# Low parts of the first block's weights on GpSimd instead of VectorE, in a two-block float32 network

## The chip, the cores and the metric

The kernel runs on one core of a Trainium2 chip. The metric is the time on the device in microseconds (us), from the start to the end of one execution. The core has TensorE (matrix products), VectorE (DVE), ScalarE (ACT), GpSimd (POOL) and SyncE (SP). Each works through its own queue in order; they wait for one another by semaphores. SBUF is the memory on chip, PSUM holds the results of TensorE.

## The reference

Two blocks of two layers each, on 512 tokens of width 1024, in float32. The change touches the first block alone. A layer of it is:

```python
h = rms_norm(x, norm_g)
z = h @ w_in
(fq, fk, fv, ff, f_gate, glu_in, c_gate,
 nq, nkc, nvc, nks, nvs, nkw, nvw, n_gl, n_gate) = jnp.split(z, split_points, axis=-1)
o_a = fox_attention(...) * jax.nn.silu(f_gate)
o_b = conformer_conv(...) * jax.nn.silu(c_gate)
o_c = nsa_attention(...) * jax.nn.silu(n_gate)
mixed = jnp.concatenate([o_a, o_b, o_c], axis=-1)
return x + mixed @ w_out
```

`fox_attention` is causal softmax attention with a decay; `conformer_conv` has 31 taps on each of 256 channels; `nsa_attention` has three branches, one over compressed keys and two of plain softmax. The second block (four mixers, gates and an MLP) is only of interest for what its trace shows.

## The kernel before

**Products in three passes.** TensorE multiplies in a one-pass float32 format with fewer bits. Each operand is split into a high part (rounded by a copy on ScalarE) and a low part (the difference), and a product is the sum of high x high, high x low and low x high (`three_passes`, L790: lines L794 to L796). The weights come from DRAM, so each tile of weights needs this at run time: `split_high` (L771, the copy at L775) on ScalarE and `split_low` (L777, the subtraction at L781, written to `w_low`) on VectorE, after a wait for the high part.

**The stream.** The large products of a layer, `h @ w_in` and `mixed @ w_out`, form a stream of 45 units (class `Inward`, L804): 29 of kind "z" for `w_in`, each one tile of up to 128 output rows and 1024 deep (24 matmuls), and 16 of kind "out" for `w_out`, each 512 deep (12 matmuls; s is the half of the depth, e the tile of the output). Weights have three slots. `fetch` (L761) on ScalarE's queue waits until the unit that used the slot is multiplied, then loads; `split_high(i + 1)` comes right behind the fetch of unit i + 2. TensorE waits for `w_low(i)` and for its PSUM bank, which VectorE's `drain` (L930; L942 for "z", L938 for "out") or, for rows with rotary embedding, the first step of `rotate_dve` (L725) frees.

**Woven with the mixers.** A unit is cut into pieces of two steps of depth. Each engine's program of the stream is a Python generator that is advanced one piece at a time (`go_on`, L637). `Stage.beside` (L324) writes a mixer's instructions into the same five queues, and after each step of the mixer's TensorE program, by a share that the mixer names, a piece of the stream. So VectorE's queue holds mixers' instructions and the stream's in the order in which they were written, and one that waits holds up all behind it. The mixers are Fox (with `Taps`: the convolution's taps on VectorE, L1614, four instructions at a step), then `ConvAndCompress`, then `Nsa`. After Nsa the rest of the stream (the second half of "out") runs by `finish` (L651), which writes each engine's remaining program to its end.

**GpSimd.** In the first block the mixers give it only two small products a layer (L1998, after waits for TensorE at L1958). The stream's `pool` (L798) yields once for each piece and then writes `total_pool` (L382): six adds at L389 that sum the squares of x (made by ScalarE at L380 as the last units are drained). TensorE sums the total over partitions (L393, L395), ScalarE makes the root (L407, L409), and a barrier ends the layer.

**Lines used below.** L562/L565 `gained_dve`: low parts of h. L744 `row_lo`. L1492: masking and maximum of Fox's scores, from PSUM. L1508: copy of transposed probabilities from PSUM. L1658: Fox's output of a tile. L1716: Fox's last transposes. L2033: GELU's scaling in the compression. L1350: low parts of the MLP's hidden values in the second block, on GpSimd. L3186, L3192, L3795: GpSimd's products in the second block's mixers. L2880: taps of the second block, on VectorE.

Of the kernel before, what the change touches and what calls it, by code (L numbers as in the profile page):

```python
# [8 lines left out]
F32 = mybir.dt.float32  # L9
F32R = mybir.dt.float32r  # L10
ACT = mybir.ActivationFunctionType
ALU = mybir.AluOpType
# [245 lines left out]
class Stage:  # L258
# [43 lines left out]
    def act(self):  # L302
        yield

    def dve(self):
        yield

    def pool(self):
        yield
# [296 lines left out]
class Woven(Stage, Gained):  # L606
# [170 lines left out]
    def split_low(self, i):  # L777
        if i < len(self.units):
            s, n, d = i % self.SLOTS, self.width(i), self.depth(i)
            self.v.wait_ge(*self.w_high(i))  # L780
            self.v.tensor_tensor(self.wl[s][:, 0:d, 0:n], self.w[s][:, 0:d, 0:n], self.wh[s][:, 0:d, 0:n].bitcast(F32),  # L781
                                 ALU.subtract).then_inc(self.w_low.sem, 1)
# [21 lines left out]
class Inward(Woven):  # L804
# [60 lines left out]
    def pe(self):  # L865
# [25 lines left out]
                yield  # L891
        self.root.sum_total_pe()

    def act(self):
        self.gained_act(range(2))
        self.split_high(0)
        self.gained_act(range(2, KD))
        for i, (kind, s, e) in enumerate(self.units):
            if kind == "z":
                yield  # L900
                self.fetch(self.a, i + 2)
                self.split_high(i + 1)
                if self.is_form(i - 2, "rope"):
                    self.row_high(i - 2)
                if self.is_form(i - 1, "split"):
                    self.row_high(i - 1)
                yield
                yield
                yield
                if i == self.kept - 1:  # L910
                    yield
            else:
                if e == 0:
                    for j in range(4):
                        self.a.copy(self.k.yT_low[:, 8 + 4 * s + j, :], self.k.yT[:, 4 * s + j, :]).then_inc(self.y_high.sem, 1)
                self.fetch(self.a, i + 2)
                self.split_high(i + 1)
                if s == 1 and e >= 2:
                    self.x_square(i - 2)
                yield  # L920
                yield
        for i in (-2, -1):
            self.x_square(len(self.units) + i)
        self.root.root_act()
# [19 lines left out]
    def dve(self):  # L944
        self.gain_dve(self.l)
        self.root.eps_dve()
        self.gained_dve(range(2))
        self.split_low(0)
        self.gained_dve(range(2, KD))
        for i, (kind, s, e) in enumerate(self.units):  # L950
            if i != 0 and i != self.kept:
                self.drain(i - 1)
            if kind == "z":
                yield
                yield
                self.split_low(i + 1)
                if self.is_form(i - 2, "rope"):
                    self.row_lo(i - 2)
                if self.is_form(i - 1, "split"):
                    self.row_lo(i - 1)  # L960
                yield
                self.rotate_dve(i - 1)
                yield
                if i == self.kept - 1:
                    self.drain(i)
                    yield
            else:
                if e == 0:
                    for j in range(4):
                        self.v.wait_ge(*self.y_high(s, j))  # L970
                        self.v.tensor_tensor(self.k.yT_low[:, 4 * s + j, :], self.k.yT[:, 4 * s + j, :],
                                             self.k.yT_low[:, 8 + 4 * s + j, :].bitcast(F32), ALU.subtract).then_inc(self.y_low.sem, 1)
                yield
                self.split_low(i + 1)
                yield
        self.drain(len(self.units) - 1)
        yield
# [2877 lines left out]
```

## Time and profile before

| | |
|---|---|
| Median of 3 runs | 3767.71 us (3763.28 to 3783.55) |
| The profiled execution | 3757.45 us, of which the span is 3755.6 us |
| Busy, share of the span | PE 92%, PEld 75%, DVE 56%, ACT 39%, POOL 11% |
| First block | 27 to 943 us, two passes (487 us is the border) |
| Mean of a 512-column matmul (L795) | 403 ns, overlapping the next |
| Units in the plain stream | 5.60 us apart ("z"), 2.80 us ("out"), by the starts of L942 and L938 |
| L1614, 128x512, first block | 120 recorded, mean 742 ns |

Times in the profile are us from the span's start. A row in order of time gives the start, the duration, the engine and line, out<-in, and in brackets how long the engine stood still before it and what ended that. A group gives busy time and the mean of one, then the engine's idle time before such instructions. Shares are means over stages with different limits.

### The profile page before, as it was taken

The numbers are of one execution on the slowest core, as the hardware profiler recorded it, in microseconds if no ns is written. First come the engines' busy times: TensorE is split into PE (matmuls) and PEld (weight loads), VectorE is DVE, ScalarE is ACT, GpSimd is POOL, SyncE is SP. The second block draws the span as 40 slices with busy tenths as digits, with TensorE's granted clock in tenths as the row PEclk, the third lists the DMA queues.
The fourth block names the chain that finished last, engine by engine and source line by source line (L and its number), as shares of the span: only waits on it lengthen the run. The fifth ranks groups of instructions, "written<-read, shape, count | busy, mean of one in ns | idle before, by whom it ended". The sixth has DMA issues, their size and how long they took to land. (4 is left out here: it accounts for less than half of the span.)

```text
span 3755.6 us, 48507 instructions
## 1 busy us (share of the span) xinstructions
PE 3441.2 (92%) x17756; PEld 2834.1 (75%) x17756; DVE 2089.3 (56%) x4082; ACT 1448.7 (39%) x2809; POOL 407.1 (11%) x322
## 2 busy tenths in 40 slices
PE   8889888898898998899999999899998999999998
PEld 6777767787587887677777887687887777777886
DVE  3756638466368883555763333478873656653333
ACT  3224332143444453444434232344453444433222
POOL 0000000000022221000202111032220000212111
PEclk9989999899899999999999999999999999999999
DMA  5633056330333323432433332433225242433332
GB/s 145 182 96 97 26 143 177 95 80 26 105 113 96 90 87 84 107 100 77 127 104 86 94 96 79 126 104 102 85 79 123 71 104 88 114 110 86 96 96 84
DMA packets 570478, 373.52 MB, mean 99 GB/s; under 512 B 77020, under 2 KB 500956, under 8 KB 569980
## 3 DMA queue, kind: packets, MB, share of 16 engines
q10 hardware_dynamic: 416768, 209.74, 20.4%
q1 hardware_dynamic: 153468, 160.59, 15.3%
q8 instruction: 148, 2.42, 0.3%
q14 instruction: 94, 0.77, 0.1%
HBM read 310.69 MB, written 59.57 MB: 99 GB/s over the span
## 5 line engine op out<-in xcount | busy, mean ns | idle before, releaser
L794 PE MATMUL bank<-h,w_hi 128*128 128x512 f32 (+2 forms) x2240 | 961.7, 429 | 124.9 <-DVE w_low L781 62.8
L796 PE MATMUL bank<-h,w_low 128*128 128x512 f32 (+2 forms) x2240 | 903.1, 403 | 0.0
L795 PE MATMUL bank<-h,w_hi 128*128 128x512 f32 (+2 forms) x2240 | 902.8, 403 | 0.0
L775 ACT CAST w_hi<-w 128x1024 fp32r<-128x1024 f32 (+2 forms) x456 | 434.4, 953 | 825.5 <-PE bank L796 661.2
L781 DVE TENSOR_TENSOR w_low<-w,w_hi 128x1024 fp32r<-128x1024 f32 (+2 forms) x456 | 507.9, 1114 | 395.2 <-ACT w_hi L775 395.0
L794 PEld LDWEIGHTS bank<-h,w_hi 128*128 128x128 f32 (+2 forms) x2240 | 430.9, 192 | 254.2 <-issue 87.6
L796 PEld LDWEIGHTS bank<-h,w_low 128*128 128x128 f32 (+2 forms) x2240 | 429.1, 192 | 107.7
L795 PEld LDWEIGHTS bank<-h,w_hi 128*128 128x128 f32 (+2 forms) x2240 | 431.7, 193 | 100.0 <-issue 13.0
L795 PE MATMUL bank<-yT_low,w_hi 128*128 128x512 f32 x768 | 305.4, 398 | 0.0
L1465 ACT ACTIVATE prob<-bank,softmax_stat 128x512 f32<-128x512 f32 (+3 forms) x256 | 144.9, 567 | 281.3 <-DVE softmax_stat L1499 204.4
L362 PE MATMUL bank<-v_tok,prob_T 128*128 128x64 f32 (+1 forms) x1376 | 188.3, 270 | 4.8 <-DVE y_tok L2154 2.1
L362 PEld LDWEIGHTS bank<-v_tok,prob_T 128*128 128x128 f32 x1376 | 176.3, 192 | 14.6 <-issue 10.7
L794 PE MATMUL bank<-yT_low,w_hi 128*128 128x512 f32 x384 | 157.6, 410 | 22.4 <-DVE xT L938 12.0
L1266 DVE TENSOR_TENSOR xT<-xT,bank 128x512 f32<-128x512 f32 x80 | 55.1, 688 | 216.9 <-PE bank L796 216.9
L795 PEld LDWEIGHTS bank<-yT_low,w_hi 128*128 128x128 f32 x768 | 146.2, 190 | 30.4
L1499 DVE TENSOR_REDUCE softmax_stat<-bank 128x1 f32<-128x128 f32 (+1 forms) x192 | 103.3, 552 | 104.3 <-PE bank L1425 103.9
L796 PE MATMUL bank<-yT_low,w_low 128*128 128x512 f32 x384 | 154.3, 402 | 0.0
L1273 DVE SCALAR_TENSOR_TENSOR relu<-bank,rstd 128x512 f32<-128x512 f32 x64 | 44.1, 692 | 185.4 <-PE bank L796 172.4
L3037 ACT COPY yT<-bank 128x512 f32<-128x512 f32 x96 | 56.3, 587 | 218.4 <-PE bank L2954 218.4
L3186 POOL TENSOR_TENSOR LT<-AT,gdn_tables 128x512 f32<-128x512 f32 x80 | 116.6, 1476 | 179.1 <-PE bank L2954 178.9
L1436 PE MATMUL bank<-tables,prob 128*128 128x128 f32 x688 | 122.2, 281 | 8.4 <-DVE prob L3335 8.3
L3790 POOL TENSOR_TENSOR weights<-weights,tables 128x128 f32<-128x128 f32 x64 | 36.4, 604 | 804.1 <-ACT weights L3710 804.1
(414 smaller groups left out, 5787.2 us busy)
## 6 DMA issues: line engine op xcount, KB each, us to landing
w<-in_w_in ACTq DMA_DIRECT2D x144, 512.0 KB, 4.2
w<-in_w_mlp ACTq DMA_DIRECT2D x128, 512.0 KB, 4.0
w<-in_w_gate ACTq DMA_DIRECT2D x64, 512.0 KB, 4.2
z<-z_tile SPq DMA_DIRECT2D x110, 256.0 KB, 4.4
w<-in_w_branch ACTq DMA_DIRECT2D x64, 256.0 KB, 2.9
z_hi<-row_part_high SPq DMA_DIRECT2D x54, 256.0 KB, 2.0
z<-z_tile_low SPq DMA_DIRECT2D x54, 256.0 KB, 2.3
k_hi<-z_hi SPq DMA_DIRECT2D x36, 256.0 KB, 6.4
```

The costliest lines, as they stand in the source:

```text
L362: m = tensor.matmul(out, l, r, start=n == 0, stop=n == len(terms) - 1)
L775: self.a.copy(self.wh[s][:, 0:d, 0:n], self.w[s][:, 0:d, 0:n]).then_inc(self.w_high.sem, 1)
L781: self.v.tensor_tensor(self.wl[s][:, 0:d, 0:n], self.w[s][:, 0:d, 0:n], self.wh[s][:, 0:d, 0:n].bitcast(F32), ALU.subtract).then_inc(self. ...
L794: self.t.matmul(bank[0:n, :], wh, high, start=j == 0, stop=False)
L795: self.t.matmul(bank[0:n, :], wh, low, start=False, stop=False)
L796: return self.t.matmul(bank[0:n, :], wl, high, start=False, stop=j == self.depth(i) - 1)
L1266: self.v.tensor_tensor(x, x, bank[:, :], ALU.add).then_inc(self.drained.sem, 1)
L1436: mm = self.t.transpose(dst[:, i * P:(i + 1) * P], src[:, i * P:(i + 1) * P], self.k.tab("ident"))
L1465: self.a.activation(self.prob[new % 3][m][:, 0:W], self.scores[c % self.score_banks][:, 0:W], ACT.Exp, bias=nmax, scale=1.0, accum_out=rsu ...
L1499: self.v.tensor_reduce(nmax, S[:, 0:W], AX.X, ALU.max, negate=True).then_inc(self.maxed.sem, 1)
L3037: a.copy(flat(buf["X"][d]), bank[2 + 2 * d][:, :]).then_inc(self.X_made.sem, 1)
L3186: p.tensor_tensor(buf["LT"][d], buf["AT"][d], self.level("levlow" if d else "levup", s), ALU.mult).then_inc(self.L_made.sem, 1)
```

## The change

`Inward` gets a `split_low` and a `pool` of its own. `split_low` does the same subtraction with the same waits and the same semaphore, on GpSimd. `pool` writes the low part of unit 0 first, then, at the second piece of each unit i, that of unit i + 1, then `total_pool` at its end as before. The three calls in VectorE's program go. `Through`, the stream of the second block, keeps `Woven.split_low` on VectorE.

```diff
--- before.py
+++ after.py
@@ -891,6 +891,23 @@
                 yield
         self.root.sum_total_pe()
 
+    def split_low(self, i):
+        if i < len(self.units):
+            s, n, d = i % self.SLOTS, self.width(i), self.depth(i)
+            self.p.wait_ge(*self.w_high(i))
+            self.p.tensor_tensor(self.wl[s][:, 0:d, 0:n], self.w[s][:, 0:d, 0:n], self.wh[s][:, 0:d, 0:n].bitcast(F32),
+                                 ALU.subtract).then_inc(self.w_low.sem, 1)
+
+    def pool(self):
+        self.split_low(0)
+        for i in range(len(self.units)):
+            yield
+            self.split_low(i + 1)
+            for _ in range(self.pieces(i) - 1):
+                yield
+        yield
+        self.root.total_pool()
+
     def act(self):
         self.gained_act(range(2))
         self.split_high(0)
@@ -945,7 +962,6 @@
         self.gain_dve(self.l)
         self.root.eps_dve()
         self.gained_dve(range(2))
-        self.split_low(0)
         self.gained_dve(range(2, KD))
         for i, (kind, s, e) in enumerate(self.units):
             if i != 0 and i != self.kept:
@@ -953,7 +969,6 @@
             if kind == "z":
                 yield
                 yield
-                self.split_low(i + 1)
                 if self.is_form(i - 2, "rope"):
                     self.row_lo(i - 2)
                 if self.is_form(i - 1, "split"):
@@ -971,7 +986,6 @@
                         self.v.tensor_tensor(self.k.yT_low[:, 4 * s + j, :], self.k.yT[:, 4 * s + j, :],
                                              self.k.yT_low[:, 8 + 4 * s + j, :].bitcast(F32), ALU.subtract).then_inc(self.y_low.sem, 1)
                 yield
-                self.split_low(i + 1)
                 yield
         self.drain(len(self.units) - 1)
         yield
```

## Rows read from the trace of the kernel before

**Rows 1.** Stretches: us busy (count) of PE, PEld, DVE, ACT, POOL; TensorE clock, DMA

```profile
487.00:943.00 456.00, 406.14 (x2196) 337.99 (x2196) 268.77 (x649) 151.02 (x330) 8.26 (x8) 0.94 0.40 107
627.00:668.00 41.00, 34.28 (x173) 27.87 (x173) 40.87 (x83) 11.82 (x23) 0.00 (x0) 0.95 0.37 109
```

**Rows 2.** Waits, 27 to 948 us: who waited for whom, us in total, times, longest

```profile
PE bank L794 <- DVE w_low L781: 21.2, 10, 5.0
...
PE bank L794 <- DVE row_part L725: 16.2, 6, 4.4
```

**Rows 3.** Groups by form, VectorE, 27 to 948 us: busy us, mean ns, idle before

```profile
L781 DVE TENSOR_TENSOR w_low<-w,w_hi 128x1024 fp32r<-128x1024 f32 x56 | 68.3, 1220 | 20.4 <-ACT w_hi L775 20.4
...
L781 DVE TENSOR_TENSOR w_low<-w,w_hi 128x512 fp32r<-128x512 f32 x32 | 21.9, 686 | 6.4 <-ACT w_hi L775 6.4
```

**Rows 4.** Groups by form, GpSimd, the whole span

```profile
L1350 POOL TENSOR_TENSOR hidden_lo<-relu,hidden_hi 128x512 fp32r<-128x512 f32 x32 | 41.4, 1294 | 227.2 <-ACT hidden_hi L1193 227.2
...
L3795 POOL TENSOR_TENSOR o_gate<-o_gate,mlstm_gain 128x1024 f32<-128x1024 f32 x4 | 9.6, 2411 | 0.0
```

**Rows 5.** Order of time, end of the second pass, by engine: start us, us

```profile
933.40 4.17 POOL L389 TENSOR_TENSOR yT<-yT 128x512 f32<-128x512 f32 x3 [1.21 <-ACT yT L380]
...
930.32 0.69 DVE L781 TENSOR_TENSOR w_low<-w,w_hi 128x512 fp32r<-128x512 f32 x1 [0.51 <-ACT w_hi L775]
931.91 0.69 DVE L938 TENSOR_TENSOR xT<-xT,bank 128x512 f32<-128x512 f32 x1 [0.91 <-PE bank L796]
932.82 0.69 DVE L781 TENSOR_TENSOR w_low<-w,w_hi 128x512 fp32r<-128x512 f32 x1 [0.22 <-ACT w_hi L775]
...
937.62 1.12 PE L393 MATMUL bank<-yT,tables 128*128 128x512 f32 x2
938.92 1.13 PE L395 MATMUL bank<-yT,tables 128*128 128x512 f32 x2 [0.18 <-ACT yT L380]
```

**Rows 6.** Order of time, second block, GpSimd and VectorE

```profile
1107.14 3.60 POOL L3186 TENSOR_TENSOR LT<-AT,gdn_tables 128x512 f32<-128x512 f32 x2 [4.66 <-PE bank L2954]
...
1106.03 0.75 DVE L2880 SCALAR_TENSOR_TENSOR qkv<-qkv_padded,qkv_taps,qkv 128x512 f32<-128x512 f32 x1
...
1107.83 3.46 DVE L2880 SCALAR_TENSOR_TENSOR qkv<-qkv_padded,qkv_taps,qkv 128x512 f32<-128x512 f32 x2
...
1131.70 2.95 POOL L3186 TENSOR_TENSOR LT<-AT,gdn_tables 128x512 f32<-128x512 f32 x2 [2.50 <-PE bank L2954]
...
1133.45 0.68 DVE L725 TENSOR_TENSOR row_part<-bank,rope_tables 128x512 f32<-128x512 f32 x1
```

**Rows 7.** Order of time, Fox of the second pass, early waits

```profile
546.42 1.05 ACT L775 CAST w_hi<-w 128x1024 fp32r<-128x1024 f32 x1 [0.44 <-DMA w<-in_w_in]
...
552.88 0.69 DVE L942 TENSOR_TENSOR z_tile<-bank,rstd 128x512 f32<-128x512 f32 x1 [5.71 <-DMA yT<-rows]
...
554.76 0.64 PE L794 MATMUL bank<-h,w_hi 128*128 128x512 f32 x1 [5.02 <-DVE w_low L781]
...
596.50 0.50 PE L794 MATMUL bank<-h,w_hi 128*128 128x512 f32 x1 [1.52 <-DVE w_low L781]
```

**Rows 8.** Order of time, Fox of the second pass, VectorE without a pause

```profile
655.73 1.05 ACT L775 CAST w_hi<-w 128x1024 fp32r<-128x1024 f32 x1 [0.44 <-DMA w<-in_w_in]
...
665.20 1.21 DVE L781 TENSOR_TENSOR w_low<-w,w_hi 128x1024 fp32r<-128x1024 f32 x1
666.33 0.27 DVE L1658 SCALAR_TENSOR_TENSOR y_tok<-bank,softmax_stat,yT 128x64 f32<-128x64 f32 x1
...
666.46 0.50 PE L794 MATMUL bank<-h,w_hi 128*128 128x512 f32 x1 [3.41 <-DVE w_low L781]
...
668.26 1.06 PE L1716 MATMUL bank<-tables,y_tok 128*128 128x128 f32 x4
```

**Rows 9.** Order of time, Conv of the second pass

```profile
730.76 1.05 ACT L775 CAST w_hi<-w 128x1024 fp32r<-128x1024 f32 x1 [0.25 <-issue]
...
733.54 0.23 DVE L2033 TENSOR_SCALAR hid_gelu<-hid_gelu 128x124 f32<-128x124 f32 x1
```

## The prediction

> **What bounds the kernel now.** I read in this order: the busy shares, then the table of stretches for the first block, then its waits, then the order of time at the places where TensorE stands still. The first block is two passes of one program, 27 to 487 us and 487 to 943 us; only these contain the changed code. In the second pass TensorE is busy 406.14 of 456 us [rows 1], so the most that any relief of other engines can give is about 50 us a pass, and most of that has other causes. What the change aims at is small. Over both passes matmuls waited 21.2 us for a low part of the weights, ten times, and 16.2 us for the rotation of a row, which is late because VectorE works through its queue in order [rows 2]. The reader should see two more things. From 627 to 668 us VectorE is busy 40.87 of 41 us [rows 1]: it is the engine that sets the pace while Fox's softmax and the convolution's taps run. And at the end of a pass GpSimd's sum of squares (L389) is what TensorE's last matmuls wait for [rows 5].
>
> **What is removed.** VectorE loses 56 low parts of 128x1024 at 1220 ns and 32 of 128x512 at 686 ns [rows 3], and two narrow ones: 68.3 + 21.9 = 90 us of VectorE over both passes. Most of it hides already: outside Fox VectorE idles while it waits for TensorE, so an instruction less only makes that wait longer. With these instructions go their waits for the high part, which hold up mixers' work in VectorE's queue.
>
> **What is added.** GpSimd gets the same subtractions. For 512 columns with the same output type it takes 1294 ns (L1350); for 1024 columns the nearest row is a multiply of 2411 ns (L3795) [rows 4]. I take 1.29 and 2.41 us. The second lies between 1.22 us (VectorE's own time) and 2.58 us (twice 1.29), and only Fox and Conv feel where. GpSimd's queue in the first block holds only k_cmp's two products per pass and the sum of squares. A low part is thus made when its high part is, and no longer when VectorE comes to it.
>
> **The end of a pass: the one certain cost.** L389's six adds follow, in GpSimd's program, all 45 low parts. Now they run between the last units: three are done before 932, the last three take 4.17 us from 933.40, end at 937.57, and L393 starts at 937.62 [rows 5]. Afterwards none can start before the last low part. Its high part is there at 932.82, so GpSimd ends it at 932.82 + 1.29 = 934.11. Then six adds of 1.29 with 0.14 us between them (4.17 = 3 x 1.29 + 2 x 0.15): 6 x 1.29 + 6 x 0.15 = 8.6, so 942.7. That is 5.1 us later, and nothing covers it: L393, L395, the root on ScalarE and the barrier follow one another. L395 no longer waits its 0.18 us for ScalarE [rows 5]: -0.2. TensorE then idles 5 us before L393. After a wait of 5.02 us a matmul took 0.64 us [rows 7] against a mean of 0.40 (the table), the mark of the 1.2 GHz level; if the two pairs of 1.12 us (1.13) are caught by it they cost up to 2.2 us more, and 0 if not; I take 0.8. Last, the pace of the units before: VectorE's low part starts at 930.32 and ends at 931.01, the unit running ends at 931.91 [rows 5]. GpSimd's would end at 931.61, 0.3 us before, less the weight load. I take 0.3 us for the seven units (bounds 0 and 1). Sum: 5.1 - 0.2 + 0.8 + 0.3 = 6.0 us per pass (5 to 8).
>
> **The shared port.** This is the cost that the trace shows in another stage. A tap of the second block takes 0.75 us alone; while GpSimd runs two L3186 from 1107.14, two taps take 3.46 us [rows 6]. The taps wait until GpSimd's instruction ends, and GpSimd in turn for the tap before it. An instruction with one input from PSUM does not wait: L725 took 0.68 us at 1133.45 with GpSimd at work [rows 6]. Two in a row take about 1.41 alone (they start 0.66 apart), so one collision cost VectorE (3.46 - 1.41) / 2 = 1.03 us for a GpSimd instruction of 1.29, so for one of 2.41 I estimate 1.03 + 1.12 = 2.15 us. In a stretch where VectorE does taps (two SBUF inputs) without pause, a low part moved away gives 1.13 us (1.22 less the overlap) and takes 2.15: a loss of 1.0 us, not a gain. The Trainium skill says the same more strictly and speaks against the change (SBUF — State Buffer, "Who interferes with whom"): a VectorE instruction with two SBUF inputs and a GpSimd one that reads SBUF exclude each other for the whole instruction. By it a collision costs the full 2.41 us, which over five collisions a pass would add 2.6 us to my sum; the rows above agree in kind and show slightly less.
>
> **Fox, about 130 us of each pass.** Step by step, for the second pass; the first has the same gaps to within 0.4 us.
> - 554.76: TensorE waits 5.02 us for a low part whose high part was ready at 546.42 + 1.05 = 547.5. VectorE was waiting for a DMA and did, at 552.88, the drain L942 and then the low part [rows 7]. The low part becomes early, but the drain frees TensorE's bank and stays behind the DMA: 552.88 + 0.69 = 553.57 is next. Gain 1.1.
> - 596.50: a wait of 1.52 us for a low part [rows 7]. Here the high part itself is late, by a DMA, and GpSimd's 1.2 us more per low part eat what its earlier start gives. Gain 0 to 0.5, taken 0.2.
> - The rotations (16.2 us over both passes, six waits of up to 4.4 us [rows 2]; the larger two of a pass are in the taps): before each of those two one low part goes from VectorE's queue (-1.13) and before each GpSimd blocks a tap or an L729 once. They come 1.2 earlier to 1 later. I take 0.
> - 666.46: TensorE waits 3.41 us for a low part started at 665.20 although its high part was ready at 655.73 + 1.05 = 656.8 [rows 8]. It becomes early. But from 627 to 668 four low parts leave VectorE (-4.5 us) and four or five holds of GpSimd come (+8.6 to +10.8, less what falls beside PSUM work, about a fifth: 7 to 8.6). The last output L1658, at 666.33 in VectorE's queue just after that low part, comes 2.5 to 4 us later, and Fox's last transposes on TensorE wait for it; they had 668.26 - 666.60 = 1.7 us of slack [rows 8]. So the gain of 3.4 becomes a loss of 1 to 2.5, taken 1.8. The low part before it also comes 1 to 2 us later, because its high part sits behind a softmax step on ScalarE that waits for VectorE: taken 1.2.
> Sum: -1.1 - 0.2 + 0 + 1.8 + 1.2 = +1.7 us per pass, with bounds of -5 (no collisions: all of the 10 us of waits a pass but what the drain keeps) and +5.
>
> **Conv.** GELU's two short scalings (L2033, 0.23 us) have one SBUF input. The first stands at 733.54 and a high part is made at 730.76 + 1.05 = 731.8 [rows 9], so a low part on GpSimd covers 731.8 to 734.2. Whether this form waits no row of mine settles; 0 if not, 0.7 to 1.9 us if so, and TensorE needs both. I take 1.0 per pass.
>
> **Nsa and the plain stream.** VectorE reads PSUM in nearly all of the softmax, and idles before the next step after each removed low part: 0. In the plain stream a unit takes 5.6 us (the table) and cast plus low part 1.05 + 2.41: covered. At the start of a pass 40 idle matmuls cover the first two low parts: 0.
>
> **Sum.** 2 x (6.0 + 1.7 + 1.0) = +17.4 us. Against the profiled execution, 3757.45 us, that is 3774.9. The median of the runs shown is 3767.71, 10.3 us above the profiled one; I expect the median to move by the same amount: 3785.1 us, or +0.46%. Differences under 0.5% (18.8 us) are about what cannot be told from no change here, so the forecast lies just inside "no change".
>
> **The rivals.**
> - *VectorE's relief wins in Fox.* GpSimd gets the port only when VectorE stands still, or collisions are few; low parts are early and the 3.41 us and half of the rotations' waits go: Fox -4, Conv 0, the end +6, hence 2 x 2 = +4 us: 3772. For it: 21.2 us of waits name the low part. Against: the 41 us without a pause. Chance 0.2.
> - *The saturated stretch decides* (slower by over 0.5%). The mechanism of the port in Fox between 627 and 668 us: every one of five holds costs its 2.15 and falls on taps: +6.2 us in VectorE, +4.5 on TensorE, Conv +1.5, the end +7: 2 x 13 = +26: 3794. It decides from about four full holds per pass on. Chance 0.27.
> - *The program doesn't run free.* GpSimd's two k_cmp products wait for TensorE (L1958) in the same queue. If a low part is queued behind such a wait it starts late, but TensorE reaches that matmul at least half a unit (2.8 us) before it needs the low part, so at most 1 us a pass: 3787. Chance 0.03.
> - *Faster by over 0.5%.* It would need over 15 us per pass in Fox to outweigh the end, where the waits for low parts and rotations are together 37.4 / 2 = 18.7 [rows 2]. Chance 0.04.
>
> **How the numbers follow.** The forecast's own case (+10 to +24) has the remaining 0.46; about a quarter of it lies above +18.8. Slower: 0.27 + 0.12 = 0.39; faster 0.04; within 0.5%: 0.57. The range runs from the first rival to beyond the second, with the spread of a median of few runs: 3768 to 3802.
>
> **What would show it.** Right: L389's adds all after the last low part, L393 at 5 us or more behind the last unit's matmul; L1614's mean well over the 742 ns of the table; low parts on GpSimd of 2.4 to 3 us; the wait at 666 gone and Fox's L1716 later. Wrong: L1614 still at 742 ns, or the end unchanged.

## The result, and the profile after

| | before | after |
|---|---|---|
| Median | 3773.38 us (3760.34 to 3792.37, 20 runs) | 3792.04 us (3773.65 to 3820.19, 20 runs) |
| Ratio after to before | | 1.0056, 95% interval 1.0041 to 1.0071 |
| The profiled execution | 3757.45 us, span 3755.6, mean clock 0.966 | 3793.81 us, span 3792.0, mean clock 0.957 |
| Busy, whole span | DVE 2089.3, POOL 407.1, PE 3441.2 us | DVE 2057.8, POOL 586.0, PE 3468.8 us |

The changed kernel is 18.7 us slower by the medians; 17.4 were forecast. Its median stands at 3792.0 us where 3785.1 was forecast (range 3768 to 3802), since that of the kernel before, 3767.71 in three runs, is 3773.38 in twenty. The interval of the ratio has 0.5% inside it, so this does not tell "no change" from "slower by over 0.5%". Eight more runs gave 3792.14 us beside 3772.34 (ratio 1.0045, interval 1.002 to 1.0069). The ratios in this document are those on record with the runs; they are not the ratios of the medians, and differ from them by up to 0.2%. That the sum is right doesn't say that its terms are. The term for Fox was off, and a whole further cause was missing.

First the operations themselves, groups by form over both passes (busy us, mean ns of one, then idle before). They answer to [rows 3, 4].

```profile
L898 POOL TENSOR_TENSOR w_low<-w,w_hi 128x1024 fp32r<-128x1024 f32 x56 | 137.0, 2446 | 367.9 <-ACT w_hi L775 367.9
L898 POOL TENSOR_TENSOR w_low<-w,w_hi 128x512 fp32r<-128x512 f32 x32 | 41.6, 1299 | 345.6 <-ACT w_hi L775 345.6
L1628 DVE SCALAR_TENSOR_TENSOR yT<-glu_padded,taps,yT 128x512 f32<-128x512 f32 x120 | 106.5, 945 | 0.0
```

The low parts cost 2.45 and 1.30 us (2.41 and 1.29 assumed). L1628 is the tap, L1614 before: its mean rose from 742 to 945 ns, 24.4 us over 120 taps. VectorE nevertheless has 31.5 us less to do over the whole span: the 90 us taken away are partly eaten by what GpSimd holds up (24.4 us on the taps, 17.8 on L744, 4.4 on L729; the scalings below are stretched too).

The end of the second pass, in order of time. It answers to [rows 5].

```profile
962.43 1.29 POOL L898 TENSOR_TENSOR w_low<-w,w_hi 128x512 fp32r<-128x512 f32 x1 [1.21 <-ACT w_hi L775]
963.67 8.37 POOL L389 TENSOR_TENSOR yT<-yT 128x512 f32<-128x512 f32 x6
...
966.74 0.40 PE L796 MATMUL bank<-yT_low,w_low 128*128 128x512 f32 x1
972.09 2.07 PE L393 MATMUL bank<-yT,tables 128*128 128x512 f32 x2 [4.96 <-POOL yT L389]
973.96 1.92 PE L395 MATMUL bank<-yT,tables 128*128 128x512 f32 x2
```

The six adds run after the last low part, and TensorE stands still for 4.96 us (5.04 in the first pass) where it had 0.14 (0.01). The four matmuls behind this take nearly twice as long as before. The next rows are stretches (from and to, length, busy us and count of PE, PEld, DVE, ACT, POOL, then the granted clock, the DMA share and GB/s): from L393 to the next pass the clock is 0.50, that is the 1.2 GHz level throughout.

```profile
500.50:512.20 11.70, 3.78 (x4) 1.18 (x4) 0.17 (x2) 3.15 (x4) 0.00 (x0) 0.50 0.09 8
```

From the end of the last unit's matmul to the next pass's first matmul takes 16.8 us, where before it took 10.4: +6.4 in the first pass. In the second, up to the following block, 29.6 against 23.2: again +6.4.

Now the stages ahead of it. The first two rows are Fox and Conv together (from a pass's start to the first matmul of w_out's units) in the kernel before, the next two those of after.

```profile
27.70:303.10 275.40, 246.22 (x1132) 197.35 (x1132) 155.22 (x288) 73.49 (x123) 0.51 (x2) 0.92 0.55 149
487.20:760.50 273.30, 243.52 (x1132) 195.08 (x1133) 155.03 (x286) 73.10 (x123) 0.51 (x2) 0.94 0.55 150
```

```profile
27.10:304.40 277.30, 246.12 (x1133) 197.22 (x1133) 148.92 (x258) 73.44 (x124) 71.13 (x32) 0.92 0.55 148
512.20:785.40 273.20, 244.07 (x1132) 195.37 (x1133) 147.24 (x256) 72.78 (x123) 70.58 (x32) 0.93 0.57 150
```

Fox and Conv took the same time to within their scatter (274.4 us on average before, 275.3 after; with a second trace of each taken in, 274.4 and 274.7). What lies behind them did not. These are Nsa's stretches, from that first matmul to 22.5 us ahead of the end of the pass's last unit: before, then after.

```profile
303.10:454.30 151.20, 134.57 (x968) 121.97 (x969) 103.46 (x350) 65.59 (x190) 0.00 (x0) 0.96 0.17 42
760.50:915.00 154.50, 137.89 (x968) 124.64 (x969) 103.59 (x350) 65.66 (x190) 0.00 (x0) 0.94 0.16 40
```

```profile
304.40:473.00 168.60, 152.50 (x970) 137.79 (x971) 99.12 (x341) 65.64 (x190) 11.59 (x9) 0.85 0.15 38
785.40:944.60 159.20, 142.96 (x969) 129.52 (x970) 98.83 (x341) 65.70 (x190) 10.96 (x9) 0.91 0.15 39
```

The same matmuls (x968 to x970) take 17.4 and 4.7 us longer, and nothing waits more: span less PE's busy time is 16.6 us in the first two rows and 16.1 and 16.2 in the other two. All of it is the clock, 0.85 and 0.91 in place of 0.96 and 0.94. The prediction had put Nsa at 0. So four questions went to the chip: what the end costs, what the port costs, whether Nsa's loss belongs to the change, and what starts it.

### The profile page after: what moved, and what is told of

Its sections match the earlier page's. It is cut to its first block and busy times, and to the rows that moved or that the text cites. A ratio compares the mean times of both kernels' runs of the same rounds, so it can differ in the third digit from the quotient of the medians.

```text
span 3792.0 us, 48507 instructions
## 1 busy us (share of the span) xinstructions
PE 3468.8 (91%) x17756; PEld 2856.0 (75%) x17756; DVE 2057.8 (54%) x3992; ACT 1448.4 (38%) x2809; POOL 586.0 (15%) x412
## 3 DMA queue, kind: packets, MB, share of 16 engines
q1 hardware_dynamic: 153468, 160.59, 15.2%
## 5 line engine op out<-in xcount | busy, mean ns | idle before, releaser
L781 DVE TENSOR_TENSOR w_low<-w,w_hi 128x1024 fp32r<-128x1024 f32 (+2 forms) x366 | 417.3, 1140 | 367.3 <-ACT w_hi L775 367.1
L795 PE MATMUL bank<-yT_low,w_hi 128*128 128x512 f32 x768 | 309.5, 403 | 0.0
L898 POOL TENSOR_TENSOR w_low<-w,w_hi 128x1024 fp32r<-128x1024 f32 (+2 forms) x90 | 179.9, 1999 | 758.9 <-ACT w_hi L775 758.9
L362 PEld LDWEIGHTS bank<-v_tok,prob_T 128*128 128x128 f32 x1376 | 178.8, 194 | 13.6 <-issue 9.6
L794 PE MATMUL bank<-yT_low,w_hi 128*128 128x512 f32 x384 | 161.4, 420 | 22.5 <-DVE xT L955 12.0
```

The lines of the kernel that those rows point to most:

```text
L362: m = tensor.matmul(out, l, r, start=n == 0, stop=n == len(terms) - 1)
L794: self.t.matmul(bank[0:n, :], wh, high, start=j == 0, stop=False)
L795: self.t.matmul(bank[0:n, :], wh, low, start=False, stop=False)
L898: self.p.tensor_tensor(self.wl[s][:, 0:d, 0:n], self.w[s][:, 0:d, 0:n], self.wh[s][:, 0:d, 0:n].bitcast(F32), ALU.subtract).then_inc(self. ...
```

## The experiments

Times of every run scatter with TensorE's mean granted clock. Over all runs of all kernels below, each kernel with a level of its own and one slope for all, the time falls by 3.5 us for each 0.001 of mean clock, and single runs then lie within 3.2 us (standard deviation) of that line. I use it to split a kernel's difference of mean times from the kernel before into "clock" (its difference of mean clock times that slope) and "work" (the rest, with its 95% interval). The kernel before is here the mean of all its runs; in the three batches that the kernels below were timed in, its means were 3770.9, 3771.8 and 3772.5 us. The idle time and the half-speed matmuls of one place fall in both parts; the split says where to look, not what caused it.

| kernel | median us (runs) | before beside it | ratio, 95% interval | work | clock |
|---|---|---|---|---|---|
| after (both batches) | 3792.0 (28) | | | +3.0 ± 1.7 | +18.4 |
| late_adds | 3779.74 (12) | 3772.34 | 1.0039 (1.0021 to 1.0056) | +5.2 ± 2.0 | +5.3 |
| adds_between | 3785.62 (9) | 3772.34 | 1.0033 (1.0007 to 1.0059) | -2.1 ± 2.3 | +12.1 |
| out_only | 3779.83 (11) | 3772.34 | 1.0028 (1.0011 to 1.0046) | +2.4 ± 2.1 | +7.5 |
| z_only | 3785.65 (12) | 3771.75 | 1.0039 (1.0022 to 1.0056) | -0.8 ± 2.1 | +13.1 |
| fox_stretch | 3781.66 (12) | 3771.75 | 1.0020 (1.0003 to 1.0037) | -0.7 ± 2.0 | +9.3 |
| not_stretch | 3780.77 (12) | 3771.75 | 1.0022 (1.0007 to 1.0038) | -1.9 ± 2.1 | +12.2 |
| filled_before | 3755.53 (11) | 3773.14 | 0.9964 (0.9951 to 0.9977) | -1.9 ± 2.1 | -13.3 |
| shifted_before | 3770.62 (11) | 3773.14 | 0.9993 (0.9978 to 1.0009) | -0.1 ± 2.0 | -1.0 |
| filled_between | 3764.45 (12) | 3773.14 | 0.9984 (0.9967 to 1.0002) | -1.7 ± 1.9 | -3.4 |
| filled_both | 3770.79 (12) | 3773.14 | 0.9994 (0.9981 to 1.0006) | -1.7 ± 1.9 | +0.6 |

Below, "in all" is work plus clock: the difference of the means. Its 95% interval is much wider than that of work, since the clock scatters: about ± 4.4 us for after, ± 2.9 to ± 5.7 for most others, ± 8.8 for adds_between.

**The end by itself (late_adds).** Before, with one wait more in GpSimd's program:

```diff
     def pool(self):
         for _ in range(self.begins[-1] + 1):
             yield
+        self.p.wait_ge(*self.w_low(len(self.units) - 1))
         self.root.total_pool()
```

> The kernel before with one wait more: GpSimd's six adds of the sum of squares start only after the last low part of a pass, which VectorE still makes. No low part moves. Theory 'the end of the pass': the last low part ends at 472.7 us in the trace of before, six adds of 1.29 us with 0.15 us between them end at 481.3, so the first matmul of the sum comes 4.5 us later per pass; and the trace of the changed kernel has 17.1 us at the 1.2 GHz level there where before has 6.8, so with slower matmuls some 5 to 7 us per pass: +10 to +14 us over both. Theory 'the port and the mixers': the cost lies where VectorE and GpSimd meet, the end is cheap because the root and the barrier have slack: within 3 us of before.

Measured +7.4 us by the medians, +10.5 in all. The order of time at the end of its second pass:

```profile
935.66 8.38 POOL L389 TENSOR_TENSOR yT<-yT 128x512 f32<-128x512 f32 x6 [187.75 <-DVE w_low L781]
...
944.10 2.07 PE L393 MATMUL bank<-yT,tables 128*128 128x512 f32 x2 [4.44 <-POOL yT L389]
945.97 1.91 PE L395 MATMUL bank<-yT,tables 128*128 128x512 f32 x2
```

The wait of 4.44 us is the expected 4.5, and the matmuls behind it are slow as in the changed kernel. The rival, that the root and the barrier have slack, falls: no low part has moved, and a cost of the size forecast for the end is there.

**The adds put back between the low parts (adds_between).** All low parts stay on GpSimd. In GpSimd's program of the changed kernel, `add_pool(j)` being step j of `total_pool`:

```diff
             self.split_low(i + 1)
+            if self.units[i][1] == 1 and self.units[i][2] >= 3:
+                self.root.add_pool(self.units[i][2] - 2)
...
-        self.root.total_pool()
+        self.root.add_pool(KD - 2)
```

> The changed kernel (all low parts on GpSimd) with the six adds put back between the low parts of the last units, in the order in which the squares become ready. Theory 'the end of the pass': the wait ahead of the first matmul of the sum (5.0 us in the changed kernel) falls to under 0.7, and of the +19 us some 12 to 14 go: +4 to +8 us on before. Theory 'the port and the mixers': it stays at +15 us or more.

```profile
953.91 1.30 POOL L910 TENSOR_TENSOR w_low<-w,w_hi 128x512 fp32r<-128x512 f32 x1 [0.35 <-ACT w_hi L781]
955.17 1.29 POOL L395 TENSOR_TENSOR yT<-yT 128x512 f32<-128x512 f32 x1
...
956.41 1.30 POOL L910 TENSOR_TENSOR w_low<-w,w_hi 128x512 fp32r<-128x512 f32 x1
957.67 4.14 POOL L395 TENSOR_TENSOR yT<-yT 128x512 f32<-128x512 f32 x3
...
961.86 1.13 PE L399 MATMUL bank<-yT,tables 128*128 128x512 f32 x2 [0.73 <-POOL yT L395]
```

The wait fell to 0.73 us and the first matmuls of the sum are back at 1.13 us. The time is 13.3 us above before by the medians and 10.0 in all; +4 to +8 had been expected if the end was nearly everything. Neither theory: the end's part went (after is +21.4 in all, so 11.4 ± 9.6 went; of work alone 5.1 ± 2.5), and some 10 us that are neither the end nor work stay. This is the first hint at the missing cause.

**Only w_out's low parts moved (out_only)**, those of Nsa and the end. In this kernel and in z_only, fox_stretch and not_stretch below, a test on the unit chooses the engine, and where the engine changes the first one waits for the other's last low part.

> Low parts on GpSimd only in the 16 narrow-depth units of each pass (w_out, 128x512), which run in Nsa and at the end; the 29 of w_in stay on VectorE; the adds follow the last low part as in the changed kernel. Theory 'the end of the pass': +10 to +14 us on before, nothing in Fox or Conv. Theory 'the port and the mixers': under +5 us. If moving low parts out of VectorE's queue during Nsa did something to that stage (157 to 166 us in the changed kernel's trace, 150 to 153 before), it shows here as well.

+7.5 us by the medians, +9.9 in all; the wait at the end is 4.97 us. That is late_adds within its interval: the 16 low parts that move in Nsa and at the end cost nothing more that shows. Its Nsa took 151.2 and 161.6 us.

**The changed kernel again (after_again).**

> The changed kernel once more, beside the others. +19 us on before (16 to 24). The question is Nsa: its first pass took 166 us at a mean granted clock of 0.86 in the changed kernel's trace against 150 us at 0.97 before. If this belongs to the change it stands here again (over 160 us); if it is the chance of one execution, it comes out between 150 and 158.

```profile
302.20:471.80 169.60, 153.38 (x970) 139.04 (x971) 99.01 (x341) 65.61 (x190) 11.60 (x9) 0.86 0.15 37
784.50:953.10 168.60, 152.56 (x970) 137.88 (x971) 99.08 (x341) 65.55 (x190) 11.62 (x9) 0.85 0.14 38
```

Nsa is long in both passes: it was not the chance of one execution.

**Only w_in's low parts moved (z_only)**, Nsa's own and the end's left on VectorE:

```diff
+    def by_pool(self, i):
+        return i < self.kept
```

> Low parts on GpSimd for the 29 units of w_in of each pass, VectorE keeps the 16 of w_out (those of Nsa and the end), and the adds run between the last units as before. The end then costs nothing. So far Nsa took 151 to 155 us per pass in the two kernels whose low parts are all on VectorE, and 159 to 170 us in six passes with all of them on GpSimd, with 12 to 19 us against 29 to 49 us at the 1.2 GHz level. Theory 'GpSimd's low parts in Nsa itself slow it': Nsa 151 to 155 us here, total within 4 us of before. Theory 'Nsa's clock hangs on what came before it (Fox and Conv shifted)': 159 to 170 us, total +8 to +16.

+13.9 us by the medians, nearly all of it clock. Nsa, in which nothing differs from the kernel before but one wait of VectorE's for GpSimd's last low part about its start, took 165.7 and 165.6 us. So what lengthens Nsa comes from ahead of it, as the second theory said.

**Only the five low parts that meet the taps (fox_stretch: units 18 to 22), and only the others of w_in (not_stretch).**

> Low parts on GpSimd only for units 18 to 22 of each pass, whose low parts meet the taps of Fox's convolution, where VectorE works without pause; all others on VectorE, adds as before. Theory 'port': each of four collisions costs VectorE 2.13 us and saves it 1.22, so Fox's last output comes about 3.6 us later, the stretch costs 1 to 3 us a pass: +2 to +6 us in all, and the tap beside GpSimd takes 2.86 us. Theory 'relief': the wait of 3.4 us at 666 us goes: -4 to -8.

> The reverse: low parts on GpSimd for the units of w_in other than 18 to 22; those and the w_out ones on VectorE, adds as before. Theory 'port': nothing is lost where VectorE has pauses and the wait at 554 us shrinks by 1: -2 to +1 us in all, if Nsa's clock is left alone. Theory 'relief': it loses what the stretch would have gained, 0 to +2.

Both are slower than before by about the same: +9.9 and +9.0 us by the medians. Neither total came out as expected, since both also lose on the clock (Nsa 168.3 and 165.8 us, 169.4 and 168.4 us); of "work" both show nothing beyond -0.7 and -1.9, so on port against relief in the total they decide little. Together the two would make 19, and z_only, which is both at once, has 13.9; a gap of 5 is within the scatter of three such differences. Moving five low parts a pass is enough for 9.3 us of the clock's loss, where z_only has 13.1. The port, though, is plain in their traces. This is fox_stretch, second pass:

```profile
674.66 2.37 POOL L910 TENSOR_TENSOR w_low<-w,w_hi 128x1024 fp32r<-128x1024 f32 x1 [0.69 <-ACT w_hi L781]
675.16 4.41 DVE L1645 SCALAR_TENSOR_TENSOR yT<-glu_padded,taps,yT 128x512 f32<-128x512 f32 x4
679.75 2.72 DVE L1645 SCALAR_TENSOR_TENSOR yT<-glu_padded,taps,yT 128x512 f32<-128x512 f32 x4
```

Four taps take 2.72 us, and 4.41 where a low part on GpSimd overlaps their start.

**The kernel before again (before_again).**

> The kernel before once more, for a second trace. Total 0 by all theories. The question is Nsa in its two passes: 151 to 155 us again if the kernel before keeps TensorE's clock there, some of them 159 to 170 if both kernels know both lengths and only their share differs.

3772.03 us, ratio 1.0001. Its Nsa took 151.2 and 160.8 us: both kernels know longer ones. Over all traces without idle matmuls at Nsa's start, the six with w_in's low parts moved in whole or part (two of them the changed kernel) have twelve passes from 159 to 170 us, the middle ones 168; the kernels without (before twice, late_adds, out_only, shifted_before below) have ten passes from 151 to 162, the middle ones 153. The ranges overlap at their ends only. By the granted clock TensorE spent 24 to 47 us of Nsa's two passes at the 1.2 GHz level in the five traces without, and 78 to 98 us in the six with; in Fox and Conv it was 74 to 79 us in the five and 68 to 79 in the six. So the clock was lost in Nsa. How much is less sure: the five traced executions were on average 8 us faster than the mean of their kernels, the six 3 us slower. Nsa's two passes together differ by 25 us between the two groups of traces; if these 12 lay in Nsa too, 13 are left, which agrees with the table.

**What starts it: the wait at Nsa's start.** TensorE's work in the 30 us ahead of Nsa is the same in both kernels, 3.15 us idle in two waits of 1.07 and 2.08 us (with one of 1.60 more in some passes). The second is for Fox's output; here before, then after:

```profile
303.15 0.47 PE L794 MATMUL bank<-yT_low,w_hi 128*128 128x512 f32 x1 [2.08 <-DVE yT_low L971]
```

```profile
304.36 0.62 PE L794 MATMUL bank<-yT_low,w_hi 128*128 128x512 f32 x1 [2.08 <-DVE yT_low L986]
```

The first matmul already takes 0.47 us in one and 0.62 in the other. The 20 us from there, second pass, of before and of after:

```profile
760.50:780.50 20.00, 17.91 (x119) 16.18 (x120) 13.19 (x41) 8.54 (x26) 0.00 (x0) 0.91 0.79 183
```

```profile
785.40:805.40 20.00, 19.99 (x90) 18.61 (x91) 8.20 (x25) 5.54 (x18) 1.27 (x1) 0.57 0.70 169
```

So two more kernels put five idle matmuls into that wait, one on the kernel before (filled_before) and one on adds_between (filled_between). As a control, shifted_before puts the same five in front of the last unit of w_in, which delays Nsa and leaves the wait. In TensorE's program, each alone:

```diff
+            if i == self.kept - 1:
+                self.keep_turning(5)      # shifted_before
...
+                    if e == 0 and j == 0:
+                        self.keep_turning((5, 0)[s])      # filled_before, filled_between
                     if e == 0:
                         self.t.wait_ge(*self.y_low(s, j))
```

> The kernel before with five idle matmuls (0.39 us each, 1.95 us) put on TensorE into the 2.08 us in which it waits, at the start of Nsa, for the first low part of Fox's output. No low part moves. So far TensorE's clock fell to the 1.2 GHz level within 1.2 us of Nsa's start in the long passes and not before 16 us in the short ones, with the same work ahead of it (3.15 us idle in the 30 us before). Theory 'Nsa's clock starts from that wait': with the wait filled Nsa takes 150 to 152 us in both passes, the mean clock rises to 0.964 or more: 4 to 8 us faster than before. Theory 'Nsa's clock hangs on its own pace, or on where the low parts are made': no change beyond 2 us.

```profile
301.06 0.50 PE L794 MATMUL bank<-yT_low,w_hi 128*128 128x512 f32 x1 [0.65 <-DVE yT_low L973]
```

The first 20 us of Nsa in its second pass:

```profile
759.00:779.00 20.00, 17.95 (x121) 16.27 (x122) 13.48 (x42) 8.57 (x26) 0.00 (x0) 0.94 0.82 190
```

3755.53 us, 17.6 below the kernel before and beyond the 4 to 8 expected: the version that beats both. The wait is 0.65 us, the clock over the first 20 us of Nsa 0.94, and Nsa took 152.7 and 154.8 us. That is no shorter than in the trace of before, whose two passes were among its good ones; the gain shows in the medians and in the mean clock (0.966 against 0.962 over all runs of before), and no trace shows where in the other executions it lies.

> The kernel before with the same five idle matmuls, but ahead of the last unit of w_in, where TensorE is busy: everything after it, Nsa's start included, comes 1.95 us later, and the wait of 2.08 us stays. No low part moves. Theory 'when Nsa starts against the chip's clock control decides' (and the change only moved that moment): Nsa takes 159 to 170 us in most passes, total +12 to +25 us, of which 4 are the matmuls themselves. Theory 'the low parts on GpSimd slow Nsa': Nsa 151 to 155, +4 us.

-2.5 us by the medians, interval -0.22% to +0.09%. The theory that any move of Nsa's start costs the clock falls: this delay of five matmuls cost nothing, Nsa took 159.5 and 154.4 us.

> All low parts on GpSimd, the adds between the last units (as in adds_between), and the five idle matmuls in the wait at Nsa's start. Theory 'Nsa's clock starts from that wait': Nsa 150 to 152 us, the 13 us that adds_between lies above before go, and what GpSimd really gives in Fox and Conv shows: -2 to -10 us on before. Theory 'the low parts on GpSimd slow Nsa': +8 us or more, Nsa 159 to 170.

3764.45 us: 15.2 us in all less than adds_between (± 9.4), as filled_before is 15.2 below before (± 2.9). That the two agree to the tenth is chance. The clock in Nsa's first 20 us is now as in filled_before:

```profile
767.40:787.40 20.00, 17.94 (x124) 16.47 (x125) 13.38 (x43) 9.05 (x28) 2.56 (x2) 0.96 0.76 186
```

So the wait does start a slow stretch, in both kernels, and filling it pays in both. But filled_between stays 10.1 ± 4.4 us in all above filled_before, about what adds_between has on before (10.0). The wait is thus not, or not alone, what makes the changed kernel's clock worse. The trace shows where the rest sits now, not why: Nsa took 162.6 us in its first pass, with 13.7 us at the 1.2 GHz level in one piece from 79 us after Nsa's start on, and 152.9 in the second.

> As filled_between, and seven more idle matmuls (2.7 us) in the wait of 3.11 us ahead of the first unit of w_out's second half, after which 10.2 us at the 1.2 GHz level stand in every trace so far. Theory 'waits of 2 to 4 us start those stretches': the stretch of 10.2 us shortens to 0 to 6.8 and 2 to 5 us per pass are won on filled_between. Theory 'the wait of 3.8 us ahead of it is enough by itself': it stays at 10.2 us and the total is that of filled_between within 2 us.

3770.79 us, 4.1 ± 4.6 us in all above filled_between: no gain, and a loss that isn't clear of the scatter. The wait of 3.11 us became 1.81, and the stretch at the 1.2 GHz level stayed at 10.2 us as the second theory said. Filling a wait is not good in itself.

## Why the prediction was right, and where it was not

**The end of a pass, forecast +6.0 a pass: right.** The trace of after has +6.4 in both. The steps held one by one: adds after the last low part (8.37 us, forecast 8.6), L393 5.0 us behind the last unit (forecast 5.1). The clock's part was too small: 0.8 was taken, with 2.2 as its bound, and the four matmuls lost 0.95 + 0.79 = 1.7 us. The pace of the units before it lost nothing that shows (0.3 taken). Late_adds gives +10.5 ± 5.7 us over both passes, and the step from after to adds_between 11.4 ± 9.6, against 12.0; the traces are the sharper evidence.

**The shared port, forecast 2.15 us for a collision: right as a price.** Twelve of 120 taps stood beside a low part and took 2.79 us on average, 2.05 more than the 742 ns of the table. There were six a pass in all of Fox; four or five had been counted for the stretch without a pause. Here are two groups of four taps in the changed kernel, one with GpSimd's low part and one without:

```profile
677.48 4.84 DVE L1628 SCALAR_TENSOR_TENSOR yT<-glu_padded,taps,yT 128x512 f32<-128x512 f32 x4
679.44 2.34 POOL L898 TENSOR_TENSOR w_low<-w,w_hi 128x1024 fp32r<-128x1024 f32 x1 [12.58 <-ACT w_hi L775]
...
691.19 2.72 DVE L1628 SCALAR_TENSOR_TENSOR yT<-glu_padded,taps,yT 128x512 f32<-128x512 f32 x4
```

4.84 - 2.72 = 2.12 us. By the stricter rule of the Trainium skill (SBUF — State Buffer, "Who interferes with whom") the cost would be the whole 2.45 us; the runs show some 0.3 to 0.4 less, as the rows of the prediction did. In kind the rule holds: the taps and L744 come to an end only after GpSimd's instruction.

**Fox, forecast +1.7 a pass: its places were right, one term and with it the sum too high.** At the first wait the drain took the low part's place, as forecast: 4.35 and 3.73 us in place of 4.69 and 5.02 [rows 7], and 2.73 and 2.06 in the second trace in place of 4.48 and 4.40. The 1.52 us became 1.43. The 3.41 us at 666 went [rows 8], and three things took its place in the second pass:

```profile
678.56 0.63 PE L1450 MATMUL bank<-tables,prob 128*128 128x128 f32 x4 [1.48 <-ACT prob_T L1488]
...
681.83 0.80 PE L794 MATMUL bank<-h,w_hi 128*128 128x512 f32 x1 [2.25 <-POOL w_low L898]
...
694.16 0.66 PE L1730 MATMUL bank<-tables,y_tok 128*128 128x128 f32 x4 [1.28 <-DVE y_tok L1672]
```

1.48 + 2.25 + 1.28 = 5.0, in place of 3.41 and of 0.56 ahead of it: +1.0, where the prediction took 1.2 + 1.8 = 3.0. L1730 is the late last transpose (L1716 before); the wait for a softmax step on ScalarE wasn't in the list. This place is the term that was mis-sized. The wait for the softmax step stands in three of the eight passes traced of kernels with all of w_in's low parts on GpSimd (after, after_again, adds_between, z_only). Here is the second pass of adds_between, without it:

```profile
665.23 0.80 PE L800 MATMUL bank<-h,w_hi 128*128 128x512 f32 x1 [2.25 <-POOL w_low L910]
...
677.79 0.66 PE L1747 MATMUL bank<-tables,y_tok 128*128 128x128 f32 x4 [1.00 <-DVE y_tok L1689]
```

Over the eight passes the waits at this place sum to 2.8 to 5.0 us, 3.9 on average, beside 4.0 before: a cost of about 0 a pass, not of 3.0. The rotations, where 0 was taken, came out near that: 16.2 us over both passes before [rows 2], 13.6 and 14.4 in the two traces of the changed kernel, 16.8 and 15.9 in those of adds_between and z_only. Here after, then adds_between:

```profile
PE bank L794 <- DVE row_part L725: 13.6, 6, 2.9
PE bank L800 <- DVE row_part L731: 16.8, 6, 3.6
```

One wait more was overlooked, 0.7 us a pass for an earlier output of Fox (L1672). In all, TensorE stood idle in Fox and Conv for 57.9 to 59.5 us over both passes in the four traces of kernels whose w_in low parts are on VectorE and that have no idle matmuls there (before, before_again, late_adds, out_only), and for 60.3, 57.7, 55.1 and 55.4 us in those of after, after_again, adds_between and z_only: 1.6 us less on average. Adds_between and z_only, which have the whole change in Fox and Conv and an end that costs nothing, have -2.1 ± 2.3 and -0.8 ± 2.1 us of work. The forecast for the two stages was +5.4.

**Conv, forecast +1.0 a pass: right as a mechanism.** GELU's scaling, with one SBUF input, does wait for GpSimd. In the first pass it took 1.98 us instead of 0.23 and ended with the low part, and TensorE waited 1.60:

```profile
273.61 2.37 POOL L898 TENSOR_TENSOR w_low<-w,w_hi 128x1024 fp32r<-128x1024 f32 x1 [2.71 <-ACT w_hi L775]
...
274.08 1.98 DVE L2047 TENSOR_SCALAR hid_gelu<-hid_gelu 128x124 f32<-128x124 f32 x1
...
276.21 0.63 PE L362 MATMUL bank<-hid_gelu,cmp_w 128*128 128x62 f32 x4 [1.60 <-DVE hid_gelu L2047]
```

In the second pass of the same trace the scaling began only 0.3 us before the low part's end and cost 0.1. In the second trace of the changed kernel both passes have the wait (1.61 us), in those of adds_between and z_only none: three of eight passes, 0.6 us a pass.

**Nsa, forecast 0: wrong, and the largest miss.** The reason given, that VectorE idles there and nothing waits for the low parts, is true (out_only), and beside the point. Nsa lost on TensorE's clock, through what was moved ahead of it (z_only). By the split of the table this is some 10 to 13 us over both passes (adds_between, z_only), by the traces up to 24, since the traced executions of before had good passes. The prediction looked at the clock only at the end of a pass and took every other stretch's clock as given.

**The sum.** Forecast 12.0 + 3.4 + 2.0 + 0. Measured, in the same order: 10.5 to 11.4 for the end, -2 to 0 for Fox and Conv together, 10 to 13 for the clock in Nsa; +18.7 by the medians, +21.4 by the means of all runs. That the number came out is luck: a cost that wasn't seen stood in for a cost in Fox that wasn't there. Of the rivals, "the saturated stretch decides" (3794) has the nearest number, by the same luck, for its +4.5 a pass in Fox isn't there. "VectorE's relief wins in Fox" (3772, Fox and Conv -8 over both passes) is about as far from the -2 to 0 measured there as the forecast's +5.4. "The program doesn't run free" can be left: the low parts start 0.08 us after their high part nearly everywhere.

**Open.** Why TensorE's clock holds less well in Nsa once some of w_in's low parts are on GpSimd, with the same work in Nsa and the same waits in the 30 us ahead of it. Not the end of the pass (adds_between), not Nsa's own low parts (z_only), not the wait at its start alone (filled_between), not any delay (shifted_before). What remains is the exact timing with which Nsa is entered, which moves with every edit ahead of it. That is argued, not shown, and no run here varied it but for the one delay of shifted_before. The Trainium skill (TensorE: Matmul & The Clock Gate, "Part 1: The HAM clock gate") says that what the clock follows is looked at in steps that run free of the kernel, so that the moment at which it changes depends on where the work falls against them. The two fates behind one and the same wait agree with this. By it alone, though, every kernel should meet both fates in time, and the middle lengths of 153 and 168 us say that the edit weighs the chances, which no run here explains.

## What to carry to other kernels

When a step is moved to an engine that "has nothing to do", look first at what already stands at the end of that engine's program: here six adds of 1.3 us, waiting behind 45 moved instructions, cost 5 us twice and the clock behind it. Price a collision of VectorE and GpSimd on SBUF by about GpSimd's whole duration, and count the places where VectorE has no pause. And check the granted clock of every stage, those too in which not one instruction is changed: in a kernel bound by TensorE filling a wait of 2 us won 7 to 8 us a pass through the clock behind it, 17.6 us by the medians, nearly as much as the whole change lost, while seven more idle matmuls in a later wait won nothing.

## What was not expected of the hardware

The same 968 to 970 matmuls of Nsa, with the same idle time of about 16 us, took 151 to 170 us, by the granted clock alone (0.96 down to 0.85), and the lengths come back to the tenth: 151.1 or 151.2 us in five passes of four traces. Without idle matmuls in it, the wait with which TensorE entered Nsa was 2.08 us in all 22 passes traced. In seven passes it kept the 2.4 GHz level for the first 16 us; in twelve, all of kernels with low parts of w_in moved, it was at 1.2 GHz within 1.2 us of the first matmul, for 3 to 17 us; in three (before_again, out_only, shifted_before) it fell just ahead of that matmul or 5 us behind it. With the wait cut to 0.65 us it kept the higher level for the first 17 us in all six passes traced.

And a TENSOR_SCALAR of 0.23 us with a single SBUF input is held by GpSimd like a tap: 1.98 us. The Trainium skill (SBUF — State Buffer, "Who interferes with whom") names `tensor_scalar` among the operations that can take the shared ports, given certain conditions on its operands, and the row agrees. It is held so in three of the four passes traced of the changed kernel.
